# The low parts of the down-projection weights in the expert stage: from VectorE to GpSimd

## The chip, the cores and the metric

The kernel runs on one core of one Trainium2 chip. The metric is the device time of one execution in microseconds (us). Five engines of the core take part: TensorE (PE, its weight loads are PEld), VectorE (DVE), ScalarE (ACT), GpSimd (POOL) and SyncE (SP), which issues the weight loads. All weights are read from HBM once per use, 248 MB in all.

## The reference, cut to what matters

Two residual layers over 256 tokens of width 1024. Each has a token mixer (attention, gated linear attention, pooling) and then a channel mixer: a dense SwiGLU in layer 0, and in layer 1 a choice of 2 out of 8 experts for each token.

```python
def swiglu(h, w_gate, w_up, w_down):
    return (jax.nn.silu(h @ w_gate) * (h @ w_up)) @ w_down

def moe_ffn(h, w_router, w_e_gate, w_e_up, w_e_down):
    ...
    for e in range(N_EXPERTS):                      # 8
        y = y + combine[..., e:e + 1] * swiglu(h, w_e_gate[e], w_e_up[e], w_e_down[e])
    return y
```

An expert is 1024 -> 1408 -> 1024, all in float32. The change lies in this last stage, the loop over the experts.

## The kernel before, in words

**Two parts for each weight.** A float32 product is made from three faster ones in the format fp32r: a weight w is split into w_hi (w rounded to fp32r) and w_lo = w - w_hi, an activation likewise, and TensorE computes x_hi*w_hi + x_lo*w_hi + x_hi*w_lo (`three`, lines 946, 947 and 948). So every weight passes ScalarE once (`round_hi`, line 320: ring -> w_hi) and VectorE once (`rest_lo`, line 328: ring minus w_hi -> w_lo), and both parts go to TensorE.

**Units, loads and halves.** One expert is one unit of 12 loads, in the order of `UNIT_LOADS` (line 43): G0 U0 G1 U1 D0 G2 U2 D1 G3 U3 D2 D3. G is gate, U is up, D is down; groups 0 to 2 are three tiles wide (1.5 MB a load), group 3 is two tiles wide (1 MB). Each load has two halves, numbered j = 0 to 23, load j // 2. A half of a wide group is 128x1536 elements, one of group 3 is 128x1024. The down halves are j = 8, 9 (D0), 14, 15 (D1), 20, 21 (D2), all 128x1536, and 22, 23 (D3), 128x1024: 8 of the 24. In the text below, "half 8" is the half with j = 8, hi(8) is its rounding on ScalarE, lo(8) its subtraction.

**Buffers.** The ring holds four loads (load i lies in slot i % 4). There are three pairs of w_hi/w_lo buffers (`NSPLIT`), half j uses pair j % 3. The semaphores `hi_ready{b}`, `lo_ready{b}` and `split_used{b}` count them: ScalarE starts hi(j) when TensorE is done with half j - 3 (`split_used`), lo(j) starts when hi(j) is done (`hi_ready`), TensorE starts half j when both are done (`parts`, line 816), and SyncE issues the load that goes into a slot when the lo of the second half that lay there is done (`unit_read`, line 381).

**Order on each engine.** Each engine walks j = 0 to 23 in its own program order, expert after expert. What else an expert needs is hung between the halves by `EXPERT_AFTER` (line 55). On TensorE it stands right behind the half of that number: "scatter" (adding the previous expert's rows into xT, L917) behind 3 and 5, "tr" (transposes of the hidden rows, L928) behind 5, 11, 17 and 20, "gather" (the tokens of the next expert, L905) behind 19. On ScalarE and VectorE the same entries stand three halves later (`EXPERT_AFTER.get(j - NSPLIT)`), ahead of hi(j) and lo(j): "gu" is the SiLU (L1452) and the product with up (L1976), "tr" is the hidden rows' hi (L1458) and lo (L1981), "gather" the tokens' hi (L1433) and lo (L1953), "scatter" the addition into xT (L1965). All these VectorE instructions read one operand from PSUM. Only lo(j) (L328) reads both from SBUF.

**GpSimd** builds constants at the start and has elementwise work in the two token mixers, the largest being L1106 (128x2048). Its program ends with L1112, at 756 us. From there on it is idle.

Of the kernel before, what the change touches and what calls it, by code (L numbers as in the profile page):

```python
# [6 lines left out]
D, T, DEPTH, P = 1024, 256, 2, 128  # L7
# [15 lines left out]
DFF, NE, DE = 2816, 8, 1408  # L23
# [19 lines left out]
UNIT_LOADS = ["G0", "U0", "G1", "U1", "D0", "G2", "U2", "D1", "G3", "U3", "D2", "D3"]  # L43
NDENSE = DFF // UF
CAP = 96
PASSES = -(-T // CAP)

HALVES = 2 * len(UNIT_LOADS)
NSPLIT = 3
# [11 lines left out]
def scatter_use(r, e):  # L61

    return PASS_USES * r + (5 * e + 1 if not (isinstance(e, int) and e == NE) else PASS_USES - 2)


def turn_use(r, e, g, last=False):

    base = PASS_USES * r + 5 * e + 3
    return (g % 2, base + (g // 2 if g < 3 else (1 if last else 2)))
# [69 lines left out]
def hybrid_trunk(nc, A, out):  # L139
# [6 lines left out]
    with ctx:  # L146
        def sb(name, shape, dt=F32):
            return ctx.enter_context(nc.sbuf_tensor(name, shape, dt))
# [8 lines left out]
        def sem(name):  # L157
            if name not in sems:
                sems[name] = ctx.enter_context(nc.semaphore(name))
            return sems[name]  # L160
# [111 lines left out]
        npi = sb("npi", [P, 1], I32)  # L272
# [16 lines left out]
        def half_buffer(u, j):  # L289

            return j % NSPLIT, PERH * u + j // NSPLIT + 1

        def wait_hi(eng, u, j):
            b, n = half_buffer(u, j)
            eng.wait_ge(sem(f"hi_ready{b}"), n)
# [10 lines left out]
        def half_words(j):  # L306

            gn = GROUPS[int(UNIT_LOADS[j // 2][1])][1]
            n = gn * D // 2
            return n, (j % 2) * n  # L310
# [12 lines left out]
        def rest_lo(dve, u, j):  # L323

            b, _ = half_buffer(u, j)
            wait_hi(dve, u, j)
            words, w0 = half_words(j)
            dve.tensor_tensor(w_lo[:, b, 0:words], ring[:, (j // 2) % NSLOT, w0:w0 + words],  # L328
                              w_hi[:, b, 0:words].bitcast(F32), SUB).then_inc(sem(f"lo_ready{b}"), 1)
# [688 lines left out]
        def _(pool):  # L1018
# [43 lines left out]
            for L in range(DEPTH):  # L1062
# [38 lines left out]
                for a in range(TT):  # L1101
                    for d in range(2):
# [9 lines left out]
            pool.affine_select(out=tri, in_=tri, compare_op=ALU.is_ge, fill=0.0, base=-1, pattern=[[1, P]],  # L1112
                               channel_multiplier=-1).then_inc(sem("tri_ready"), 1)


        @block.scalar
        def _(act):
# [374 lines left out]
        def _(dve):  # L1492
# [454 lines left out]
            def tokens(r, e, n):  # L1947

                for c in range(2):
                    b, uses = gather_use(r, e - 1, c)  # L1950
                    dve.wait_ge(sem("hTe_hi_ready"), 2 * n + c + 1)
                    k = slice(4 * c, 4 * c + 4)
                    dve.tensor_tensor(hTe_lo[:, k, :], PS[:, 4 + b, 0:4 * CAP].rearrange("p (k c) -> p k c", k=4),  # L1953
                                      hTe_hi[:, k, :].bitcast(F32), SUB).then_inc(sem(f"aux_free{b}"), 1)

            def rows_out(n):
                wait_used(dve, NDENSE + n, HALVES - 1)
                dve.tensor_copy(ye[:, 512:1024], PS[0:CAP, 7, :]).then_inc(sem("ye_dve"), 1)

            def added(uses, part):  # L1960

                for c in (2 * part, 2 * part + 1):
                    wait_aux_full(dve, c % 2, uses + c // 2)
                    x = xT[:, 2 * c:2 * c + 2, :]
                    dve.tensor_tensor(x, x, two(PS[:, 4 + c % 2, :]), ADD).then_inc(sem(f"aux_free{c % 2}"), 1)  # L1965

            def expert(r, e, n, first=False, last=False):
                u = NDENSE + n
                for j in range(HALVES):
                    if j == 2 and not first:  # L1970
                        rows_out(n - 1)
                    for what, g in EXPERT_AFTER.get(j - NSPLIT, ()):
                        g0, gn = GROUPS[g]
                        if what == "gu":
                            dve.wait_ge(sem("sile_ready"), len(GROUPS) * n + g + 1)
                            dve.tensor_tensor(hide[:, g % 2, 0:gn * P], sile[:, g % 2, 0:gn * P],  # L1976
                                              PS[0:CAP, 2 * (g % 2) + 1, 0:gn * P], MUL).then_inc(sem("hide_ready"), 1)
                        elif what == "tr":
                            b, _ = turn_use(r, e, g, last)
                            dve.wait_ge(sem("hdT_hi_ready"), len(GROUPS) * n + g + 1)  # L1980
                            dve.tensor_tensor(hdT_lo[:, g0:g0 + gn, :],  # L1981
                                              PS[:, 4 + b, 0:gn * CAP].rearrange("p (k c) -> p k c", k=gn),
                                              hdT_hi[:, g0:g0 + gn, :].bitcast(F32), SUB).then_inc(sem(f"aux_free{b}"), 1)
                        elif what == "scatter" and not first:
                            added(scatter_use(r, e), g)
                        elif what == "gather" and not last:
                            tokens(r, e + 1, n + 1)
                    if not (j < NSPLIT and isinstance(n, int) and n == 0):
                        rest_lo(dve, u, j)

            def weigh():
# [16 lines left out]
            def one_pass(r):  # L2008
                n = r * NE
                for a in range(TT):  # L2010
                    dve.tensor_tensor(psel[:, a], slots[:, :].unsqueeze(1).broadcast_to([P, NE, CAP]),
                                      pos[:, a, :].unsqueeze(2).broadcast_to([P, NE, CAP]), ALU.is_equal)\
                       .then_inc(sem("psel_ready"), 1)
                if isinstance(r, int):
                    weigh()
                dve.wait_ge(sem("psel_ready"), 2 * (r + 1))
                for a in range(TT):
                    dve.tensor_tensor(wsel[:, a], psel[:, a], wt[:, a, :].unsqueeze(2).broadcast_to([P, NE, CAP]), MUL)\
                       .then_inc(sem("sel_ready"), 1)
                dve.tensor_scalar(pos[:, :, :], pos[:, :, :], float(CAP), None, SUB).then_inc(sem("pos_step"), 1)  # L2020
                dve.wait_ge(sem("pos_step"), r + 1)
                tokens(r, 0, n)
                expert(r, 0, n, first=True)
                with dve.Fori(1, NE - 1) as e:
                    expert(r, e, n + e)
                expert(r, NE - 1, n + NE - 1, last=True)
                rows_out(n + NE - 1)
                for part in range(2):
                    added(scatter_use(r, NE), part)
# [3 lines left out]
            npass = dve.value_load(npi[0:1, 0:1], min_val=1, max_val=PASSES)  # L2033
# [42 lines left out]
```

## Time and profile before

| what | value |
|---|---|
| time of three runs | 1362.99 us median (1362.39, 1362.99, 1373.96) |
| span of the profiled execution (first to last instruction) | 1360.9 us |
| median of the runs minus that span | 2.1 us |
| TensorE busy, share of the span | 1271.6 us, 93% |
| VectorE busy | 908.7 us, 67% |
| ScalarE busy | 720.9 us, 53% |
| GpSimd busy | 108.4 us, 8% |
| mean granted TensorE clock | 0.942 of full speed |

The span is that of one execution under the profiler; its own time is not listed apart from it, so the 2.1 us between the span and the median stand for what lies around the span. The experts fill the last third, from about 900 us to 1350 us. Busy time of TensorE is that of pipelined matmuls: the start of one to the start of the next is the better measure of what one costs (a 128x512 one starts 0.23 us after the one before, a 128x384 one 0.175 us).

### The profile page before, as it was taken

The numbers are of one execution on the slowest core, as the hardware profiler recorded it, in microseconds if no ns is written. First come the engines' busy times: TensorE is split into PE (matmuls) and PEld (weight loads), VectorE is DVE, ScalarE is ACT, GpSimd is POOL, SyncE is SP. The second block draws the span as 40 slices with busy tenths as digits, with TensorE's granted clock in tenths as the row PEclk, the third lists the DMA queues.
The fourth block names the chain that finished last, engine by engine and source line by source line (L and its number), as shares of the span: only waits on it lengthen the run. The fifth ranks groups of instructions, "written<-read, shape, count | busy, mean of one in ns | idle before, by whom it ended". The sixth has DMA issues, their size and how long they took to land.

```text
span 1360.9 us, 21645 instructions
## 1 busy us (share of the span) xinstructions
PE 1271.6 (93%) x8701; PEld 1170.2 (86%) x8701; DVE 908.7 (67%) x1130; ACT 720.9 (53%) x929; POOL 108.4 (8%) x126
## 2 busy tenths in 40 slices
PE   6999988998899999899988899889999999999997
PEld 6889878998899999879878899788888888888885
DVE  4538975577444454434896548658888788888884
ACT  4745733354444443654483235537666666666763
POOL 3005322000000000000731200000000000000000
PEclk8989977999999999997996689979999999999999
DMA  6443331245446544342342134629998988989982
GB/s 216 127 124 101 93 93 63 94 155 189 167 155 217 187 140 128 112 131 68 101 136 77 48 105 159 232 64 312 305 324 293 333 308 297 323 299 333 305 292 86
DMA packets 162662, 248.10 MB, mean 182 GB/s; under 512 B 4254, under 2 KB 140564, under 8 KB 162580
## 3 DMA queue, kind: packets, MB, share of 16 engines
q1 hardware_dynamic: 161328, 246.82, 54.2%
q8 instruction: 59, 0.97, 0.3%
q10 hardware_dynamic: 1252, 0.13, 0.1%
q14 instruction: 23, 0.19, 0.0%
HBM read 245.89 MB, written 1.05 MB: 181 GB/s over the span
## 4 chain that ended last, share of the span: by engine, by line
PE 77%; DVE 15%; ACT 4%; issue 3%; POOL 2%; DVEq 0%; POOLq 0%; ACTq 0%
PE PS L528 20%; PE PS L946 8%; PE PS L947 8%; PE PS L948 8%; PE PS L829 5%; PE PS L831 5%; PE PS L830 5%; PE PS L694 4%; DVE m_lo L1582 4%; PE PS L905 2%; PE PS L492 2%; DVE w_lo L328 2%; ACT w_hi L320 2%; DVE scr L1744 2%; PE PS L625 2%
## 5 line engine op out<-in xcount | busy, mean ns | idle before, releaser
L328 DVE TENSOR_TENSOR w_lo<-ring,w_hi 128x1536 fp32r<-128x1536 f32 (+1 forms) x240 | 388.0, 1624 | 152.9 <-ACT w_hi L320 151.4
L320 ACT ACTIVATE w_hi<-ring 128x1536 fp32r<-128x1536 f32 (+1 forms) x240 | 329.2, 1378 | 159.7 <-PE PS L831 85.9
L1178 ACT ACTIVATE m_hi<-ring 128x512 fp32r<-128x512 f32 (+2 forms) x256 | 156.6, 629 | 222.2 <-PE PS L528 221.8
L1582 DVE TENSOR_TENSOR m_lo<-ring,m_hi 128x512 fp32r<-128x512 f32 (+2 forms) x256 | 190.2, 772 | 115.4 <-ACT m_hi L1178 114.4
L528 PE MATMUL PS<-h_hi,m_hi 128*128 128x256 f32 (+2 forms) x672 | 202.9, 302 | 13.1 <-DVE h_lo L1590 7.1
L528 PE MATMUL PS<-h_lo,m_hi 128*128 128x256 f32 (+2 forms) x672 | 197.3, 294 | 0.0
L528 PE MATMUL PS<-h_hi,m_lo 128*128 128x256 f32 (+2 forms) x672 | 196.9, 293 | 0.0
L946 PE MATMUL PS<-w_hi,hTe_hi 128*96 128x384 f32 (+1 forms) x512 | 168.6, 329 | 6.7 <-DVE w_lo L328 5.5
L947 PE MATMUL PS<-w_hi,hTe_lo 128*96 128x384 f32 (+1 forms) x512 | 165.3, 323 | 0.0
L948 PE MATMUL PS<-w_lo,hTe_hi 128*96 128x384 f32 (+1 forms) x512 | 165.1, 323 | 0.0
L528 PEld LDWEIGHTS PS<-h_hi,m_hi 128*128 128x128 f32 (+2 forms) x672 | 134.7, 200 | 18.1 <-issue 12.3
L528 PEld LDWEIGHTS PS<-h_lo,m_hi 128*128 128x128 f32 (+2 forms) x672 | 134.5, 200 | 1.1 <-issue 0.5
L528 PEld LDWEIGHTS PS<-h_hi,m_lo 128*128 128x128 f32 (+2 forms) x672 | 134.2, 200 | 0.4
L829 PE MATMUL PS<-h_hi,w_hi 128*128 128x256 f32 x352 | 100.5, 285 | 2.8 <-DVE h_lo L1590 2.8
L830 PE MATMUL PS<-h_lo,w_hi 128*128 128x256 f32 x352 | 100.2, 285 | 0.0
L831 PE MATMUL PS<-h_hi,w_lo 128*128 128x256 f32 x352 | 100.1, 284 | 0.0
L946 PEld LDWEIGHTS PS<-w_hi,hTe_hi 128*96 128x96 f32 x512 | 82.6, 161 | 16.1 <-issue 10.0
L947 PEld LDWEIGHTS PS<-w_hi,hTe_lo 128*96 128x96 f32 x512 | 82.8, 162 | 5.9
L948 PEld LDWEIGHTS PS<-w_lo,hTe_hi 128*96 128x96 f32 x512 | 82.7, 162 | 5.1
L694 PE MATMUL PS<-selh,scr 128*128 128x2 f32 x256 | 55.1, 352 | 20.4 <-DVE scr L1744 20.4
L694 PEld LDWEIGHTS PS<-selh,scr 128*128 128x128 f32 x256 | 54.8, 332 | 21.1 <-issue 21.1
L946 PE MATMUL PS<-w_hi,hdT_hi 128*96 128x512 f32 x176 | 70.3, 399 | 0.9 <-issue 0.9
(310 smaller groups left out, 2451.0 us busy)
## 6 DMA issues: line engine op xcount, KB each, us to landing
ring<-in_w_in_dram SPq DMA_DIRECT2D x40, 1024.0 KB, 5.2
ring<-in_w_exp_gate_dram SPq DMA_DIRECT2D x24, 1536.0 KB, 7.8
ring<-in_w_exp_up_dram SPq DMA_DIRECT2D x24, 1536.0 KB, 8.3
ring<-in_w_exp_down_dram SPq DMA_DIRECT2D x24, 1536.0 KB, 7.3
ring<-in_w_branch_dram SPq DMA_DIRECT2D x12, 1024.0 KB, 5.0
ring<-in_w_ffn_gate_dram SPq DMA_DIRECT2D x6, 1536.0 KB, 6.6
ring<-in_w_ffn_up_dram SPq DMA_DIRECT2D x6, 1536.0 KB, 7.1
ring<-in_w_ffn_down_dram SPq DMA_DIRECT2D x6, 1536.0 KB, 6.4
```

The lines of the kernel that those rows point to most:

```text
L320: act.activation(w_hi[:, b, 0:words], ring[:, i % NSLOT, w0:w0 + words], ACT.Copy)\
L328: dve.tensor_tensor(w_lo[:, b, 0:words], ring[:, (j // 2) % NSLOT, w0:w0 + words], w_hi[:, b, 0:words].bitcast(F32), SUB).then_inc(sem(f"l ...
L528: mm = pe.matmul(dst, l, r, start=(kt == 0 and x == 0 and y == 0), stop=(kt == PIECES * per - 1 and y == 2), skip_group_check=True)
L694: mm = pe.matmul(bank[:, c * GH + 2 * d:c * GH + 2 * d + 2], E[:, d, c, :, :], selh[:, :], start=True, stop=True)
L829: pe.matmul(dst, whi, xhi, start=start, stop=False, skip_group_check=True)
L830: pe.matmul(dst, whi, xlo, start=False, stop=False, skip_group_check=True)
L831: return pe.matmul(dst, wlo, xhi, start=False, stop=stop, skip_group_check=True)
L946: pe.matmul(dst, xhi, whi, start=start, stop=False)
L947: pe.matmul(dst, xlo, whi, start=False, stop=False)
L948: return pe.matmul(dst, xhi, wlo, start=False, stop=stop)
L1178: act.activation(hi, raw, ACT.Copy).then_inc(sem("m_hi_ready"), 1)
L1582: dve.tensor_tensor(lo, raw, hi.bitcast(F32), SUB).then_inc(sem("m_lo_ready"), 1)
```

## The change

In the expert stage VectorE leaves out lo(j) for the down halves, and GpSimd runs a loop of its own that does just these, in the same order: lo(8), lo(9), lo(14), lo(15), lo(20) to lo(23) of each of the 8 experts. Instruction, operands, buffers and semaphores are the same (`rest_lo` is called with `pool` in place of `dve`). The dense stage isn't touched: there VectorE does all. The block `If(npass > 1)` serves a case (over 96 tokens for one expert) that these inputs don't reach.

```diff
@@ -1112,6 +1112,22 @@
             pool.affine_select(out=tri, in_=tri, compare_op=ALU.is_ge, fill=0.0, base=-1, pattern=[[1, P]],
                                channel_multiplier=-1).then_inc(sem("tri_ready"), 1)
 
+            def expert(n):
+
+                for j in range(HALVES):
+                    if UNIT_LOADS[j // 2][0] == "D":
+                        rest_lo(pool, NDENSE + n, j)
+
+            expert(0)
+            with pool.Fori(1, NE) as e:
+                expert(e)
+            pool.wait_ge(sem("passes_known"), 1)
+            npass = pool.value_load(npi[0:1, 0:1], min_val=1, max_val=PASSES)
+            with pool.If(npass > 1):
+                with pool.Fori(1, npass) as r:
+                    with pool.Fori(0, NE) as e:
+                        expert(r * NE + e)
+
@@ -1985,7 +2001,7 @@
                         elif what == "gather" and not last:
                             tokens(r, e + 1, n + 1)
-                    if not (j < NSPLIT and isinstance(n, int) and n == 0):
+                    if UNIT_LOADS[j // 2][0] != "D" and not (j < NSPLIT and isinstance(n, int) and n == 0):
                         rest_lo(dve, u, j)
```

## Rows read from the trace of the kernel before

**Rows 1.** Windows: us, busy by engine, then PEclk, DMA share, GB/s.

```profile
930.00:1361.00 431.00, 413.69 (x2395) 353.49 (x2393) 343.19 (x295) 275.56 (x267) 0.00 (x0) 1.00 0.86 293
1125.30:1180.80 55.50, 54.52 (x317) 46.74 (x318) 45.76 (x40) 36.77 (x36) 0.00 (x0) 1.00 0.91 312
```

**Rows 2.** Waits, 1125.3 to 1180.8 us: us in total, times, longest us.

```profile
ACT w_hi L320 <- PE PS L948: 9.2, 13, 1.9
DVE w_lo L328 <- ACT w_hi L320: 8.3, 16, 1.1
PE PS L946 <- DVE w_lo L328: 0.8, 1, 0.8
```

**Rows 3.** Timeline of TensorE, one expert: start us, us, [idle before <-releaser].

```profile
1125.30 0.41 PE L946 MATMUL PS<-w_hi,hTe_hi 128*96 128x384 f32 x1 [0.77 <-DVE w_lo L328]
...
1146.29 0.39 PE L946 MATMUL PS<-w_hi,hdT_hi 128*96 128x512 f32 x1
...
1150.45 0.34 PE L946 MATMUL PS<-w_hi,hTe_hi 128*96 128x384 f32 x1
...
1159.12 0.39 PE L946 MATMUL PS<-w_hi,hdT_hi 128*96 128x512 f32 x1
...
1163.29 0.28 PE L946 MATMUL PS<-w_hi,hTe_hi 128*96 128x256 f32 x1
...
1172.68 0.46 PE L946 MATMUL PS<-w_hi,hdT_hi 128*96 128x512 f32 x1
...
1174.95 0.45 PE L946 MATMUL PS<-w_hi,hdT_hi 128*96 128x512 f32 x1
...
1180.80 0.41 PE L946 MATMUL PS<-w_hi,hTe_hi 128*96 128x384 f32 x1 [0.77 <-DVE w_lo L328]
```

**Rows 4.** Timeline of VectorE, the same expert.

```profile
1144.10 3.58 DVE L328 TENSOR_TENSOR w_lo<-ring,w_hi 128x1536 fp32r<-128x1536 f32 x2 [0.92 <-ACT w_hi L320]
...
1148.38 3.52 DVE L328 TENSOR_TENSOR w_lo<-ring,w_hi 128x1536 fp32r<-128x1536 f32 x2 [0.25 <-ACT w_hi L320]
...
1156.92 3.58 DVE L328 TENSOR_TENSOR w_lo<-ring,w_hi 128x1536 fp32r<-128x1536 f32 x2 [0.46 <-ACT w_hi L320]
...
1160.89 1.21 DVE L328 TENSOR_TENSOR w_lo<-ring,w_hi 128x1024 fp32r<-128x1024 f32 x1
...
1168.38 3.43 DVE L328 TENSOR_TENSOR w_lo<-ring,w_hi 128x1536 fp32r<-128x1536 f32 x2 [0.73 <-ACT w_hi L320]
...
1176.51 1.23 DVE L328 TENSOR_TENSOR w_lo<-ring,w_hi 128x1024 fp32r<-128x1024 f32 x1 [0.59 <-ACT w_hi L320]
1178.80 3.43 DVE L328 TENSOR_TENSOR w_lo<-ring,w_hi 128x1536 fp32r<-128x1536 f32 x2 [1.06 <-ACT w_hi L320]
```

**Rows 5.** Timeline of ScalarE: hi(0) and hi(1) of the next expert.

```profile
1177.28 2.94 ACT L320 ACTIVATE w_hi<-ring 128x1536 fp32r<-128x1536 f32 x2 [0.80 <-PE PS L948]
```

**Rows 6.** GpSimd's lines by form: count | busy us, mean ns | idle before.

```profile
L1106 POOL TENSOR_TENSOR scr<-scr,gk 128x2048 f32<-128x2048 f32 x8 | 38.1, 4782 | 103.2 <-ACT scr L1339 103.2
...
L1084 POOL TENSOR_TENSOR kdec<-gk,PT 128x512 f32<-128x512 f32 x2 | 2.6, 1284 | 0.0
```

**Rows 7.** Timelines of VectorE and GpSimd, 169 to 186 us, in token mixer 0.

```profile
169.45 6.93 DVE L1582 TENSOR_TENSOR m_lo<-ring,m_hi 128x512 fp32r<-128x512 f32 x4
176.31 2.28 DVE L1766 TENSOR_TENSOR qk<-PS,chm 128x2048 f32<-128x2048 f32 x1
178.63 4.32 DVE L1744 TENSOR_TENSOR scr<-scr,gq 128x2048 f32<-128x2048 f32 x1
182.87 2.48 DVE L1582 TENSOR_TENSOR m_lo<-ring,m_hi 128x512 fp32r<-128x512 f32 x4
...
170.91 9.89 POOL L1106 TENSOR_TENSOR scr<-scr,gk 128x2048 f32<-128x2048 f32 x2 [23.00 <-ACT scr L1339]
```

**Rows 8.** DMA issues: count, KB each, median us from issue to landing.

```profile
ring<-in_w_exp_up_dram SPq DMA_DIRECT2D x24, 1536.0 KB, 8.3
```

**Rows 9.** Windows of 4 us in token mixer 0, columns as in rows 1.

```profile
170.00:174.00 4.00, 2.85 (x24) 2.85 (x25) 4.00 (x4) 3.97 (x6) 3.09 (x1) 1.00 0.80 239
...
182.00:186.00 4.00, 2.91 (x14) 2.94 (x15) 4.00 (x6) 0.00 (x0) 0.00 (x0) 0.64 0.00 0
```

## Prediction, made before the changed kernel was run

> **What bounds the kernel now.** I read the windows of the expert stage first: from 930 us to the end TensorE is busy 413.7 of 431 us at full granted clock (2.4 GHz), VectorE 343, ScalarE 276, GpSimd 0 [rows 1]. Then one expert: the first matmul of half 0 starts at 1125.30 and again at 1180.80, so an expert takes 55.50 us [rows 3]. In it TensorE waits for VectorE once, 0.77 us, ahead of half 0 [rows 2, 3]. ScalarE waits for TensorE (9.2 us) and VectorE for ScalarE (8.3 us): the loop runs TensorE done with half j-3, hi(j), lo(j), TensorE half j, and its pace is TensorE's [rows 2]. VectorE, busy 45.8 of 55.5 us, is not the bound. So there is little to win: all of TensorE's waits for lo in the stage are some 0.8 us for each expert. The question is whether lo of the down halves, slower on GpSimd, still comes before TensorE wants it.
>
> **Price of one lo on GpSimd.** No row shows this instruction there. The nearest are its two-input instructions of 128x512 (1.28 us) and 128x2048 (4.78 mean) [rows 6]. The mean of the second holds waits: two of them took 9.89 us while VectorE's m_lo ran beside them [rows 7]. Take 4.57, worked out here: in rows 7 VectorE's third m_lo ends at about 171.3, and the two GpSimd instructions and one m_lo (2.48/4 = 0.62) in between last until 170.91 + 9.89 = 180.80; (180.80 - 171.3 - 0.4)/2 = 4.55, rounded up a little. Through 512 and 2048 the line is 0.19 us plus 2.14 ns an element: p = 3.47 us for 128x1536, q = 2.38 us for 128x1024. Bounds: below, in proportion and without a fixed part, 4.57 x 1536/2048 = 3.43 and 2.29, with a little slack 3.35 and 2.25; above, 4.78 x 1536/2048 = 3.6, with slack for the output format fp32r, which no GpSimd row has, 3.75 and 2.6. On VectorE the same take 1.76 (3.52/2) and 1.22 [rows 4].
>
> **What is removed.** From VectorE 6 x 1.76 + 2 x 1.22 = 13.0 us for each expert. Its work isn't on the path, so this is worth nothing by itself. lo(0), the one for which TensorE waits, starts at 1178.80 when hi(0) is ready, 1.06 us after VectorE fell idle [rows 4], so an emptier VectorE doesn't bring it forward.
>
> **What is added, half by half.** I walk through the expert of rows 3 and 4, with everything ahead of the pair unchanged. From the end of a lo to TensorE's start is 0.23 us (lo(0), 1178.80 + 3.43/2 = 1180.5, against 1180.80, gives 0.28; I take 0.23). A down half takes TensorE 2.08 us ((1150.45 - 1146.29)/2).
>
> D0 (halves 8, 9). hi(8) is ready at 1144.10. lo(8) on GpSimd until 1147.57, TensorE starts half 8 at 1147.80 where it started at 1146.29: late by 1.51, ends 1149.88. lo(9) queues behind lo(8) and ends at 1151.04; half 9 starts 1151.27, ends 1153.35, where it ended at 1150.45. **+2.90 us** (in general 2p - 4.04).
>
> D1 (14, 15). Same pattern: hi(14) ready 1156.92, half 14 was wanted at 1159.12 (2.20 later, as 2.19 before), the pair was done at 1163.29. Now 1156.92 + 2p + 0.23 + 2.08 = 1166.17: **+2.88 us**.
>
> D2, D3 (20 to 23). Here the gather stands ahead of half 20 on TensorE and covers a part: hi(20) ready 1168.38, half 20 wanted only at 1172.68. But four lo's queue on GpSimd, until 1168.38 + 2p + 2q = 1180.08. Ends are 1171.85 (in time for half 20), 1175.32 (half 21 was wanted at 1174.95, late by 0.6), 1177.70, 1180.08; hi(23), ready at 1176.51 before, is there in time with 0.6 more. Half 23, 6 matmuls or 1.39 us, then runs from 1180.31 to 1181.70. Next is lo(0) of the next expert, on VectorE. hi(0) started at 1177.28, when half 21 was done [rows 5], and moves by 0.6, ready at 1179.35; with the lock (below) lo(0) starts when GpSimd is free, 1180.08, ends 1181.84, and TensorE starts half 0 at 1182.07 against 1180.80: **+1.27 us** (2p + 2q - 10.43). The 0.77 us of wait that was there hides a part.
>
> Sum for one expert 2.90 + 2.88 + 1.27 = 7.05 us (6p + 2q - 18.5), for eight 56.4; the last has no half 0 behind it and loses 1.8 in place of 1.27: 57.0 us. The stalls aren't made up again anywhere: TensorE has no other idle time in the expert to give back.
>
> **The shared read port.** Rows 7 show what VectorE does beside GpSimd. Four m_lo take 2.48 us alone, but 6.93 when GpSimd's 128x2048 runs: one of them was held for about 4.5 us, one whole GpSimd instruction. L1744 of 128x2048 took 4.32 us and ended at 182.95, 2.15 after GpSimd's pair had ended at 180.80. L1766, as large, with one operand in PSUM, took 2.28 beside GpSimd. So an instruction with two SBUF operands waits for the whole GpSimd instruction, and one with a PSUM operand doesn't. The Trainium skill, page "SBUF — State Buffer", section "Who interferes with whom", says just this: a VectorE instruction with two SBUF inputs and a GpSimd one that reads SBUF exclude each other for the whole instruction. By that rule, the trace agrees, only L328 is hit, not the other VectorE work of the stage. Priced: GpSimd holds the port 6p + 2q = 25.6 us for each expert, VectorE's remaining 16 lo's need 12 x 1.76 + 4 x 1.22 = 26.0 us, together 51.6 of the new 62.6 us, so the port isn't the bound. By place: lo(10), ready 1148.35, waits until 1151.04 and ends at 1152.80, wanted (with D0's delay) at 1153.35: hidden by 0.3. lo(16), ready 1160.89, waits until lo(15) is done at 1163.86, wanted 1166.17: hidden. lo(0): the 0.4 us counted above. If nothing excluded anything, the sum would be 0.4 x 8 = 3 us less.
>
> **Transfers.** Load 8 goes out when lo(9) is done, 3.4 us later than before, against 2.9 for TensorE. It lands 8.3 us on [rows 8], 1159.3; hi(16), its first reader, follows at about 1162.7. For D3's slot: 1180.08 + 8.3 = 1188.4, hi(6) is wanted from 1190.5. Covered by 2 to 3 us; DMA is busy 0.91 of the time and has more air at 62.6 us an expert. SyncE's wait in order adds nothing else.
>
> **Rivals.**
> A. VectorE gets in between two queued GpSimd instructions. In rows 7 the waiting m_lo did: GpSimd's second instruction came after it. Here VectorE's lo(10) would have to be ready before lo(8) ends (1148.35 against 1147.57, margin 0.8 us) or lo(16) before lo(14) ends (1160.89 against 1160.39, margin 0.5). Then the second lo of the pair is late by another 1.76 or 1.22 us: 3.0 x 8 = 24, 1444 us. It decides from p = 4.0 for D1, 4.25 for D0. Chance 0.15.
> B. The clock. The stalls (1.5, 1.4 us twice for each expert) could cost TensorE its full clock. For it: after 178 to 182 us, almost without a matmul, the granted clock was 0.64 in the window [rows 9], down to 1.2 GHz next. Against: with 2.85 busy of 4 us it stayed at 1.00 [rows 9]. A pair here has 2.1 us of work in 3.5. If one stretch of 8 us for each expert ran at half clock it would cost 8 x 8 = 64 us beyond the sum: 1484. Chance 0.07.
> C. GpSimd is quick enough: not slower. It decides from 1144.10 + 2p + 0.23 <= 1148.38, p <= 2.0 us, and for the last four 2p + 2q <= 10.4. Then nothing is late and nothing is won: 1363 us. The row of 4.78 at 2048, and 1.28 at only 512, speak against it. Chance 0.04; a gain of over 1% (14 us) isn't there to have, since TensorE's waits for lo are 8 x 0.8 = 6 us.
> D. Other, such as GpSimd well slower for fp32r (p = 4.2: 6 x 4.2 + 2 x 2.9 - 18.5 = 12.5 for each expert, at least 1463): 0.08.
>
> **How the numbers follow.** Forecast 0.66: the profile's span 1360.9 + 57.0 = 1417.9; the median of the runs is 2.1 us above the span, so 1363.0 + 57.0 = 1420.0. With p, q from 3.35, 2.25 to 3.75, 2.6 the loss for one expert is 6.1 to 9.2, so 1412 to 1437. The range takes in A (1444) and goes a little below for handoffs and D2's cover that I may have put too high: 1404 to 1450. B and most of D stay outside. This kernel's measurement can tell about 1% from no change: faster 0.01, same 0.04, slower 0.95.
>
> **What would show it.** GpSimd's L328 at about 3.5 us (128x1536) and 2.4 (128x1024), 64 in all, 205 us busy. TensorE's waits for GpSimd's w_lo: about 1.5, 1.4, 1.5, 1.4, then 0.6, 0.3, 1.0 us in each expert, and gather to gather 62.6 us in place of 55.5. Some of VectorE's L328 stretched to 3 or 4 us, above all the first after D0 and D1. Granted clock 1.00. Wrong it would be with a GpSimd lo far from 3.5 us, with VectorE's lo(10) or lo(16) between two of GpSimd's, or with the clock below 1.

## The result, and the profile after

| | before | after |
|---|---|---|
| median of the runs | 1362.69 us (4 runs, 1361.12 to 1373.96) | 1419.33 us (4 runs, 1417.24 to 1421.78) |
| ratio, 95% interval | | 1.0391 (1.0341 to 1.0441) |
| span of the profiled execution | 1360.9 us | 1415.2 us |
| mean granted TensorE clock | 0.942 | 0.947 |

The change costs 56.6 us (median against median). Two sections of the profile's page put it in the expert stage: the first line is busy time, share of the span and number of instructions, the other two are the span in 40 slices, in tenths. GpSimd (POOL) now works in the last third, and the granted clock (PEclk) keeps its level there.

```profile
PE 1279.6 (90%) x8701; PEld 1163.4 (82%) x8701; DVE 855.8 (60%) x1066; ACT 722.1 (51%) x929; POOL 312.1 (22%) x190
...
POOL 3006311000000000005312000053524335352533
PEclk9989977999999999989977899899999999999999
```

GpSimd's instructions from 900 us on, by form (count | busy us, mean ns | idle before):

```profile
L328 POOL TENSOR_TENSOR w_lo<-ring,w_hi 128x1536 fp32r<-128x1536 f32 x48 | 166.0, 3481 | 440.5 <-ACT w_hi L320 440.5
L328 POOL TENSOR_TENSOR w_lo<-ring,w_hi 128x1024 fp32r<-128x1024 f32 x16 | 38.0, 2400 | 0.0
```

So a lo on GpSimd takes 3.48 and 2.40 us, 1.76 and 1.22 on VectorE [rows 4]. One expert in windows (columns as in rows 1), from the first matmul of half 0 to the same one of the next expert: 62.39 us where it was 55.50.

```profile
1149.14:1211.53 62.39, 56.03 (x318) 46.40 (x318) 39.20 (x32) 36.92 (x36) 25.46 (x8) 1.00 0.79 278
```

TensorE's timeline in that expert, which answers to rows 3. Shown are the first matmuls of halves 8, 9, 10, then 14, 15, 16, then 20, 21, 23 and 0 (start us, us, [idle before <-releaser]):

```profile
1171.82 0.44 PE L946 MATMUL PS<-w_hi,hdT_hi 128*96 128x512 f32 x1 [1.54 <-POOL w_lo L328]
...
1175.06 0.45 PE L946 MATMUL PS<-w_hi,hdT_hi 128*96 128x512 f32 x1 [0.94 <-POOL w_lo L328]
...
1177.20 0.34 PE L946 MATMUL PS<-w_hi,hTe_hi 128*96 128x384 f32 x1
...
1187.30 0.44 PE L946 MATMUL PS<-w_hi,hdT_hi 128*96 128x512 f32 x1 [1.29 <-issue]
...
1190.78 0.44 PE L946 MATMUL PS<-w_hi,hdT_hi 128*96 128x512 f32 x1 [1.18 <-POOL w_lo L328]
...
1192.91 0.28 PE L946 MATMUL PS<-w_hi,hTe_hi 128*96 128x256 f32 x1
...
1202.32 0.45 PE L946 MATMUL PS<-w_hi,hdT_hi 128*96 128x512 f32 x1
...
1205.11 0.44 PE L946 MATMUL PS<-w_hi,hdT_hi 128*96 128x512 f32 x1 [0.33 <-POOL w_lo L328]
...
1209.81 0.44 PE L946 MATMUL PS<-w_hi,hdT_hi 128*96 128x512 f32 x1 [0.62 <-POOL w_lo L328]
...
1211.53 0.41 PE L946 MATMUL PS<-w_hi,hTe_hi 128*96 128x384 f32 x1
```

Half 0 began at 1125.30 before and at 1149.14 after, so 23.84 us bring the two onto one scale. Half 10 was to start at 1150.45 + 23.84 = 1174.29 and started at 1177.20: 2.91 us lost on D0. Half 16: 1163.29 + 23.84 + 2.91 = 1190.04, started 1192.91: 2.87 on D1. The next half 0: 1180.80 + 23.84 + 5.78 = 1210.42, started 1211.53: 1.11 on D2 and D3. Together 6.89 us. The idle times in brackets are a little shorter than the delay, since a matmul's record reaches past the start of its successor.

GpSimd and VectorE side by side around D0 and around D2, D3:

```profile
1167.99 6.92 POOL L328 TENSOR_TENSOR w_lo<-ring,w_hi 128x1536 fp32r<-128x1536 f32 x2 [20.71 <-ACT w_hi L320]
...
1198.05 11.62 POOL L328 TENSOR_TENSOR w_lo<-ring,w_hi 128x1536 fp32r<-128x1536 f32 x4 [7.42 <-ACT w_hi L320]
...
1172.20 5.99 DVE L328 TENSOR_TENSOR w_lo<-ring,w_hi 128x1536 fp32r<-128x1536 f32 x2 [0.82 <-ACT w_hi L320]
...
1208.98 3.98 DVE L328 TENSOR_TENSOR w_lo<-ring,w_hi 128x1536 fp32r<-128x1536 f32 x2 [3.44 <-ACT w_hi L320]
```

The queue of two runs from 1167.99 to 1174.91, and half 9 starts 0.15 us after it. lo(10) on VectorE has its operands at 1172.20 but lasts 4.32 us, until 1176.52: it is held until GpSimd is done at 1174.91 and then takes 1.6. TensorE wants it at 1177.20, so this holding is hidden. At the end of the expert lo(0), begun at 1208.98, waits for GpSimd's last (1209.67) in the same way; this one isn't hidden.

### The profile page after: what moved, and what is told of

Read it like the earlier page. It is cut to its first block, busy times and chain, and to the rows that moved or that the text cites. A ratio compares the mean times of both kernels' runs of the same rounds, so it can differ in the third digit from the quotient of the medians.

```text
span 1415.2 us, 21700 instructions
## 1 busy us (share of the span) xinstructions
PE 1279.6 (90%) x8701; PEld 1163.4 (82%) x8701; DVE 855.8 (60%) x1066; ACT 722.1 (51%) x929; POOL 312.1 (22%) x190
## 3 DMA queue, kind: packets, MB, share of 16 engines
q1 hardware_dynamic: 161328, 246.82, 51.4%
## 4 chain that ended last, share of the span: by engine, by line
PE 50%; issue 22%; POOL 14%; DVE 12%; ACT 2%; POOLq 0%; DVEq 0%; ACTq 0%
PE PS L528 20%; POOL w_lo L328 12%; PE PS L829 5%; PE PS L830 5%; PE PS L831 5%; PE PS L694 4%; DVE m_lo L1598 3%; PE PS L492 2%; DVE scr L1760 2%; PE PS L625 1%; PE PS L739 1%; DVE small L1720 1%; PE PS L501 1%; DVE Pr L1732 1%; DVE w_lo L328 1%
## 5 line engine op out<-in xcount | busy, mean ns | idle before, releaser
L328 DVE TENSOR_TENSOR w_lo<-ring,w_hi 128x1536 fp32r<-128x1536 f32 (+1 forms) x176 | 331.1, 1894 | 156.1 <-ACT w_hi L320 156.0
L328 POOL TENSOR_TENSOR w_lo<-ring,w_hi 128x1536 fp32r<-128x1536 f32 (+1 forms) x64 | 203.7, 3211 | 440.5 <-ACT w_hi L320 440.5
L1072 POOL TENSOR_TENSOR qk<-qk,rows 32x512 f32<-32x512 f32 x8 | 12.7, 1613 | 527.5 <-PE PS L656 527.5
L946 PEld LDWEIGHTS PS<-w_hi,hdT_hi 128*96 128x96 f32 x176 | 28.3, 161 | 80.1 <-issue 72.2
```

Of the source, the lines that this page charges most:

```text
L946: pe.matmul(dst, xhi, whi, start=start, stop=False)
```

## The experiments

Each time stands beside that of the kernel before on the same chip; except for the last, each is a single run. "Period" is gather to gather in the profile (first L905 of one expert to the next), 55.50 us before and 62.38 after. "Stage" is from the first gather to the end of the span. Both are read to 0.1 us where the time of a single run isn't: the first gather comes anywhere from 893 to 908 us, in code that no experiment touches, and that enters the times.

| run | time, us more than before | stage, us | more than before |
|---|---|---|---|
| kernel before | | 464.2 | |
| changed kernel | 56.6 | 522.2 | 58.0 |
| half of the instructions | 19.8 | 487.9 | 23.7 |
| only D2 and D3 | 9.4 | 475.9 | 11.7 |
| short instruction | 2.8 | 464.2 | 0.0 |
| same duration without reading | 51.4 | 517.6 | 53.4 |
| unneeded reads | 94.9 | 557.8 | 93.6 |
| unneeded writes | 1.5 | 464.1 | -0.1 |
| longer lo | 196.6 | 648.1 | 183.9 |
| half 0 in two instructions | -4.9 | 460.1 | -4.1 |

The diffs are shortened to the lines that matter. In all runs with GpSimd work but the one with only D2 and D3, its loop over the experts is also written out (`for e in range(NE)`) in place of `Fori`; with the unneeded writes this leaves the period at 55.50.

The theory: TensorE waits because the lo's of a down pair stand in one GpSimd queue, p = 3.5 us each, behind a hi that comes no earlier than before; what is lost is read from each place by what covers it. Rivals: the cost goes with GpSimd's time of work (its hold on the shared read port); the hand-over to another engine or the later release of ring slots costs; VectorE gets in between; the clock falls.

### Half of the instructions moved

```diff
-    if UNIT_LOADS[j // 2][0] == "D":
+    if UNIT_LOADS[j // 2][0] == "D" and j % 2 == 1:
```

VectorE takes the rest. GpSimd's lo(9) also waits for VectorE's lo(8) here, so that the load's slot is freed by both.

> Only the second halves of the down loads (9, 15, 21, 23) go to GpSimd, the first ones (8, 14, 20, 22) stay on VectorE. Theory (a queue of two GpSimd instructions makes the pair late): lo(8) is in time on VectorE, lo(9) starts on GpSimd with it done, 1145.9 + 3.48 + 0.23 = 1149.6 against 1148.4 wanted: 1.2 us late; D1 the same; D2's lo(21) is covered by the gather; D3 0.1. Together 2.5 us for each expert, +20 us, period 58.0 us. Rival (cost in proportion to the time that GpSimd works, because it holds the shared port or because of handing over): half of the 56.6 us measured, +28 us, spread over all four.

Measured: 1384.9 us against 1365.0, +19.8 us; period 58.26 us, 2.76 more than before. Half the instructions cost 40% of the loss of a period (and 41% of that of the stage); the rival wanted half. That is a narrow margin, and the next run separates the two better. TensorE waits for GpSimd's w_lo in 20 instances of about 0.9 us in the 390 us from 950 on (18.3 us in all).

```profile
PE PS L946 <- POOL w_lo L328: 18.3, 20, 1.2
```

These are three in an expert, by place: 1.1 us at D0, 1.1 at D1 and 0.5 at D3, where 0.1 was expected. With the first lo of a pair on VectorE, the second alone is still late: one GpSimd lo is too slow where TensorE follows at once.

### Only D2 and D3 moved

```diff
-    if UNIT_LOADS[j // 2][0] == "D":
+    if UNIT_LOADS[j // 2] in ("D2", "D3"):
```

> Only the halves 20 to 23 (D2 and D3) go to GpSimd, D0 and D1 stay on VectorE. Theory: place decides. The gather on TensorE covers most of the queue of four, so the loss is the 1.1 us measured there for each expert, +9 us, period 56.6 us. Rival (cost in proportion to GpSimd's busy time, 11.8 of 25.5 us for each expert): 46% of 56.6 us, +26 us.

Measured: 1374.4 against 1365.0, +9.4 us; period 56.56, 1.06 more than before. 46% of GpSimd's time of work causes 15% of the loss for one expert, the same 1.1 us that D2 and D3 lose in the changed kernel. Cost in proportion to GpSimd's work falls (it wanted 26 us, the stage shows 11.7); place decides. The stage's 11.7 are 7 x 1.06 and 4.3 in the last expert, which the expected +9 had left out. The queue of four is there as before:

```profile
1172.74 11.60 POOL L328 TENSOR_TENSOR w_lo<-ring,w_hi 128x1536 fp32r<-128x1536 f32 x4 [44.94 <-ACT w_hi L320]
```

### The same waits and signals with a short instruction

```diff
-    rest_lo(pool, NDENSE + n, j)
+    wait_hi(pool, NDENSE + n, j)
+    pool.memset(w_lo[:, b, 0:words].bitcast(F32), 0.0).then_inc(sem(f"lo_ready{b}"), 1)
```

> GpSimd fills w_lo of the down halves with zeros in place of the subtraction (the low parts of the down weights are left out of the result), so the same waits, signals and queue but about 1.4 us for 128x1536, write only. Theory (only the duration matters, decided at p = 2.0 us): nothing late, 1361 to 1364 us, period 55.5 us. Rival (handing over to GpSimd, or slots freed later): part of the 7 us for each expert remains.

Measured: 1367.9 against 1365.0 in one run each; period 55.53 us, that of the kernel before to 0.03. GpSimd's lines there, and TensorE's waits, which are those of the kernel before:

```profile
L1123 POOL MEMSET w_lo<- 128x1536 f32 x42 | 58.0, 1382 | 286.4 <-ACT w_hi L320 286.4
L1123 POOL MEMSET w_lo<- 128x1024 f32 x14 | 13.3, 953 | 31.0 <-ACT w_hi L320 31.0
```

```profile
PE PS L946 <- DVE w_lo L328: 5.5, 7, 0.8
```

The 2.8 us lie ahead of the experts: the stage takes 464.2 us in both profiles. So the hand-over to GpSimd costs nothing at 1.4 us, below the point of decision of 2.0 us, which itself was not tested. A later release of the ring's slots is not tested here, since a lo of 1.4 us frees them no later; it is in the next run. This one also shows that nothing is to be won: VectorE loses the down lo's, and the period stays.

### The same duration without reading

Two more memsets into the unused m_lo tile ahead of the one above, so that a lo takes 3.34 us (start to start) and 2.49 us, but GpSimd reads nothing.

```diff
+    step(pool.memset(spare, 0.0))                      # 128 x words
+    step(pool.memset(spare[:, 0:words // 1024], 0.0))  # 128 x 512
     pool.memset(w_lo[:, b, 0:words].bitcast(F32), 0.0).then_inc(sem(f"lo_ready{b}"), 1)
```

> As the one with zeros, but with two more memsets into a scratch tile ahead, so that each lo takes about 3.4 us (128x1536) and 2.4 us (128x1024) and GpSimd never reads SBUF (the low parts of the down weights are left out). Theory: the stalls of TensorE return almost whole, period 62.0 us, +54 us; only lo(0) of the next expert is no longer held, 0.4 us less for each expert, and no L328 of VectorE lasts longer than 1.8 us. Rival (the shared port is the main cause): far less, under +20 us.

Measured: 1416.4 against 1365.0, +51.4 us; period 61.73 us. The stalls are back though the port is free: VectorE's longest L328 (its durations are min/median/max in ns) is 1.76 us, against 4.33 in the changed kernel, whose row stands second.

```profile
L328 DVE TENSOR_TENSOR w_lo<-ring,w_hi x101: 1224/1758/1761, 949.4 to 1339.3; 128x1536 fp32r<-128x1536 f32 x76, 128x1024 fp32r<-128x1024 f32 x25
```

```profile
L328 DVE TENSOR_TENSOR w_lo<-ring,w_hi x99: 1211/1758/4325, 959.4 to 1338.2; 128x1536 fp32r<-128x1536 f32 x75, 128x1024 fp32r<-128x1024 f32 x24
```

The formula with these durations gives 6 x 3.34 + 2 x 2.49 - 18.5 = 6.5 us, and 6.1 with nothing held; measured 6.2. The slots are freed nearly as late here as in the changed kernel, and the formula, which has no term for that, leaves at most 0.1 us for it. Of the 6.88 us for each expert at most 0.65 are due to the port (62.38 - 61.73, of which about 0.4 is the shorter duration).

### The port alone: unneeded reads, unneeded writes

The kernel before, in which VectorE does every lo, with GpSimd working on tiles nobody uses, at the same moments.

```diff
+    wait_hi(pool, NDENSE + n, j)
+    step(pool.tensor_tensor(m_lo[:, 0:words // 512, 0:512], x, x, SUB))   # x = m_hi, in SBUF
```

> The kernel before, where VectorE does every lo, plus a GpSimd that does an unneeded subtraction of the same size, both operands in SBUF, each time hi of a down half is ready. Nobody waits for it. Theory of the shared read port: VectorE's lo(9), lo(10) and so on are held for whole GpSimd instructions of 3.5 us, TensorE becomes late by about 5 to 6 us at D0 and D1 each and at D2/D3 together, 16 us for each expert, +100 to +150 us, and L328 rows of 4 to 5 us on VectorE. Rival (no exclusion): the time of the kernel before, 1363 us.

Measured: 1456.5 against 1361.6, +94.9 us; period 66.63 us, 11.1 more. Direction and mechanism as expected, the size a third smaller: I had every GpSimd instruction hold a lo that TensorE waits for, but VectorE's lo came first each time and the two engines took turns, and at D0 two held lo's made TensorE late, 1.69 us for lo(9) and 1.87 for lo(10):

```profile
1195.05 0.44 PE L946 MATMUL PS<-w_hi,hdT_hi 128*96 128x512 f32 x1 [1.69 <-DVE w_lo L328]
...
1199.22 0.39 PE L946 MATMUL PS<-w_hi,hTe_hi 128*96 128x384 f32 x1 [1.87 <-issue]
```

The 11.1 us are waits of this kind, and nothing of them is the clock: the same two waits, to 0.04 us, stand in all eight experts, and in five of the six periods (66.62 to 66.64 us) the granted clock is 1.00. Only in the expert shown, and in the last one, did it fall right after them, here in windows of 4 us (columns as in rows 1). This period took 68.22 us, 1.6 more than the others:

```profile
1196.00:1200.00 4.00, 2.13 (x11) 1.39 (x10) 4.00 (x2) 1.48 (x1) 1.51 (x1) 1.00 0.89 261
1200.00:1204.00 4.00, 4.00 (x16) 3.51 (x15) 2.69 (x3) 1.48 (x1) 0.00 (x0) 0.59 0.52 126
```

With memsets of 1.4 + 1.4 + 0.5 us in place of the subtraction:

```diff
-    step(pool.tensor_tensor(m_lo[:, 0:words // 512, 0:512], x, x, SUB))
+    step(pool.memset(x, 0.0)), step(pool.memset(x, 0.0)), step(pool.memset(x[:, 0:words // 1024], 0.0))
```

> As the one with unneeded reads, but GpSimd's instructions are memsets of the same total duration (about 3.4 and 2.4 us), write only. Theory: only reading excludes VectorE's two-operand instructions, so 1363 us and no L328 over 1.8 us on VectorE. Rival (any GpSimd instruction blocks): again +100 us.

Measured: 1363.1 against 1361.6 in one run each; period 55.50 us, exactly that of before, and VectorE's longest L328 is 1.76 us. The exclusion is one of reads: GpSimd's reading holds VectorE's subtraction, its writing doesn't. With the waits that it sets off it is worth about 94 us where VectorE's lo's stand close to TensorE's need, and 5 us at most (8 x 0.65) in the changed kernel, where they have moved out of the way.

### A longer lo

```diff
+    step(pool.tensor_tensor(m_lo[:, 0, 0:512], x, x, SUB))    # 128x512, unneeded
     rest_lo(pool, NDENSE + n, j)
```

> The changed kernel with an unneeded GpSimd subtraction of 128x512 (1.3 us) ahead of each of its eight lo's, so p is about 4.9 and q 3.8 us. Theory by the formula alone (6p + 2q - 18.5): 18.5 us for each expert, +148 us. With VectorE getting in between (rival A of the prediction, which decides from p = 4.0 and 4.25): lo(10) and lo(16) go ahead of a queued GpSimd instruction, 3 us more, +170 us, and the timelines show an L328 of VectorE between two instructions of a GpSimd pair.

Measured: 1558.2 against 1361.6, +196.6 us, of which 183.9 are in the stage (the first gather came at 908.20 us, in place of 896.75); period 78.5 us, 23.0 more, above both numbers. The added instruction takes 1.04 us alone. From one lo to the next in the queue p is 4.5 and q 3.5, and the formula gives 6 x 4.5 + 2 x 3.5 - 18.5 = 15.5. GpSimd and VectorE at D0:

```profile
1169.62 3.45 POOL L328 TENSOR_TENSOR w_lo<-ring,w_hi 128x1536 fp32r<-128x1536 f32 x1
1173.03 2.55 POOL L1124 TENSOR_TENSOR m_lo<-m_hi 128x512 fp32r<-128x512 f32 x1
1175.66 3.44 POOL L328 TENSOR_TENSOR w_lo<-ring,w_hi 128x1536 fp32r<-128x1536 f32 x1
...
1172.71 1.97 DVE L328 TENSOR_TENSOR w_lo<-ring,w_hi 128x1536 fp32r<-128x1536 f32 x1 [0.82 <-ACT w_hi L320]
```

lo(10) is ready at 1172.71, 0.36 us before GpSimd's lo(8) ends (1173.07), and goes next: GpSimd's 128x512 takes 2.55 us in place of 1.04. That is rival A of the prediction, 1.5 us here and 1.0 at D1 (2.02 against 1.04). It occurs a third time, which neither the prediction nor this run's expectation had: at the end of the expert lo(0) of the next one goes ahead of GpSimd's last lo, which takes 3.74 us in place of 2.38.

```profile
1141.76 1.03 POOL L1124 TENSOR_TENSOR m_lo<-m_hi 128x512 fp32r<-128x512 f32 x1
1142.87 3.74 POOL L328 TENSOR_TENSOR w_lo<-ring,w_hi 128x1024 fp32r<-128x1024 f32 x1
...
1142.32 2.09 DVE L328 TENSOR_TENSOR w_lo<-ring,w_hi 128x1536 fp32r<-128x1536 f32 x1 [5.21 <-ACT w_hi L320]
```

That makes 3.9 us for rival A, less about 0.5, since half 0 no longer waits for a held lo(0). The rest, 23.0 - 15.5 - 3.4 = 4.1 us for each expert, lies with rival B. Windows of 4 us in the same expert as D0 above (columns as in rows 1):

```profile
1166.00:1170.00 4.00, 3.87 (x24) 3.61 (x25) 1.13 (x3) 3.06 (x3) 1.43 (x2) 1.00 0.87 272
1170.00:1174.00 4.00, 1.37 (x8) 0.90 (x7) 1.84 (x2) 2.08 (x3) 4.00 (x2) 1.00 0.41 164
1174.00:1178.00 4.00, 2.82 (x8) 1.36 (x6) 0.68 (x1) 1.09 (x1) 3.92 (x2) 0.53 0.00 0
1178.00:1182.00 4.00, 2.76 (x7) 1.89 (x8) 2.28 (x1) 0.40 (x1) 1.09 (x1) 0.50 0.35 86
```

After a stretch with TensorE busy 1.37 of 4 us the granted clock is at its lower level (1.2 GHz). Half 9 took 3.9 us (1179.24 to 1183.16) in place of 2.1. Read the same way from the starts of matmuls, the lower level cost 0.6 us more at the start of half 10, 1.1 in half 23 and 0.5 at the start of half 0, together 4.0 us on TensorE's path: the rest is the clock.

### A version that beats both

The short memset showed that the down lo's are not what VectorE needs relief from. TensorE's one wait for a lo in an expert is the 0.77 us ahead of half 0 [rows 3], where hi(0) and lo(0) stand in series. Without GpSimd, for experts 1 to 7:

```diff
+    # ScalarE, j == 0: two instructions of 128x768, the first signals hi_first
+    act.activation(w_hi[:, b, 0:x], ring[:, s, 0:x], ACT.Copy).then_inc(sem("hi_first"), 1)
+    act.activation(w_hi[:, b, x:words], ...).then_inc(sem(f"hi_ready{b}"), 1)
+    # VectorE, j == 0
+    dve.wait_ge(sem("hi_first"), n)
+    dve.tensor_tensor(w_lo[:, 0, 0:x], ring[:, 0, 0:x], w_hi[:, 0, 0:x].bitcast(F32), SUB)
+    wait_hi(dve, u, 0)
+    dve.tensor_tensor(w_lo[:, 0, x:2 * x], ...).then_inc(sem("lo_ready0"), 1)
```

> No GpSimd work: the kernel before, where hi(0) and lo(0) of experts 1 to 7 are each done in two instructions of 128x768, so that VectorE starts on the first part 0.7 us earlier. Theory (TensorE's only avoidable wait in the expert stage is the 0.77 us ahead of half 0, which hangs on hi(0) then lo(0) in series): lo(0) ends about 0.7 us earlier, the wait nearly goes, lo(2) still comes in time to 0.2 us, period 54.9 to 55.1 us, 3 to 5 us faster than before. Rival (TensorE is held by something else there, or lo(2) is late instead): period 55.5 us, no change.

Measured: median 1357.6 us (11 runs) against 1362.5 (16 runs), ratio 0.9962 (95% interval 0.9943 to 0.9981). The period is 54.9 us, and the wait is down from 0.8 to 0.2 or 0.3 us:

```profile
PE PS L952 <- DVE w_lo L2000: 1.5, 7, 0.3
```

So 4.9 us, 0.36%, faster than the kernel before by the medians (the interval reaches from 0.2 to 0.6%, the stage shows 4.1 us), and by the medians some 62 us faster than the changed one (1419.3).

## Why the prediction was right, step by step

**Price of one lo.** 3.47 and 2.38 us were read off a line through two other GpSimd instructions [rows 6]; 3.48 and 2.40 came out. The output format fp32r, for which the upper bound had slack, added nothing to it. Taking the held instruction's wait out of the 4.78 us [rows 7] mattered: in proportion to the mean it would have been 3.6, and 0.7 us more for each expert.

**The walk.** D0 2.90 predicted, 2.91 measured; D1 2.88 and 2.87; D2 with D3 1.27 and 1.11. The last is mis-sized by 0.16: I let lo(0) take its whole 1.76 us after GpSimd's release, but a held instruction finished 1.6 us after it, and the queue of four took 11.62 us where I had 11.70. TensorE's waits, forecast at 1.5, 1.4, 1.5, 1.4, then 0.6, 0.3 and 1.0, came at the same halves but one: 1.54, 0.94, 1.29, 1.18, then 0.33, none and 0.62 in brackets. The period was to be 62.6, it is 62.4.

**The step that failed: the last expert.** The sum gave it 1.8 us for D2 and D3 in place of 1.27, and left the cover of the gather in it. But the last expert has no gather (`not last` in the code), so nothing covers the queue of four there. TensorE's timeline of the last expert after, first matmul of halves 20 and 21 (their records say what was waited for; "issue" stands where the profile shows no releaser):

```profile
1388.75 0.44 PE L946 MATMUL PS<-w_hi,hdT_hi 128*96 128x512 f32 x1 [2.62 <-issue]
...
1392.24 0.44 PE L946 MATMUL PS<-w_hi,hdT_hi 128*96 128x512 f32 x1 [1.02 <-POOL w_lo L328]
...
1399.35 3.94 PE L917 MATMUL PS<-qk,big 96*128 96x256 f32 x16 [0.82 <-ACT big L1455]
```

From the last gate/up matmul triple's start (1385.62) to the last scatter (1399.35) are 13.7 us, before 9.6 (1335.45 to 1345.03): 4.15 us lost there, 2.3 more than in the sum.

**The sum.** Over the stage, from the first gather to the end of the span: 5.8 up to the second gather, 6 periods of 6.87 = 41.2, and 10.95 from the last gather to the end (1.1 + 2.9 + 2.9 + 4.15), 58.0 us. The span grew by 54.3 only, because the profiled execution after reached its first gather 3.7 us earlier (893.04 against 896.75 us), in code that the change doesn't touch. So 57.0 predicted stands against 58.0 in the stage and 56.6 in the medians. That 1420.0 met 1419.3 to 0.7 us is in part luck: the last expert was 2.3 us too low in the sum, the other seven together about 1 us too high, and the medians have 1.4 us less than the stage.

**Nothing gained from VectorE.** Right, and shown by the short memset, which frees VectorE of the same work and leaves the period at 55.53.

**The shared read port.** With GpSimd reading beside VectorE's lo's a period took 66.63 us, with it writing 55.50. That is how the Trainium skill, page "SBUF — State Buffer", section "Who interferes with whom", tells the two apart: a VectorE instruction with two SBUF inputs contends with a GpSimd instruction that reads SBUF, and not with one that only writes it. The prediction's "not the bound, hidden except for lo(0)" was right: 0.65 us at most.

**Transfers.** Right: median time from issue to landing even fell (7.5 us for the up weights, 8.3 before [rows 8]), and no ScalarE wait for a load stands in the expert.

**Rivals.** A did not occur in the changed kernel (GpSimd's pairs run without a gap, 6.92 us for two). But it does occur with p = 4.5, and the rule by which it decides, ready before GpSimd's current instruction ends, is seen there. It was priced at 3.0 us for each expert and cost 3.4, since lo(0) gets in as well. B did not occur either: the expert's granted clock is 1.00. It occurs with the longer lo, where it cost 4.0 us for each expert; the prediction's 8 us for one stretch at half clock came from no row. C, decided at p = 2.0, is what the short memset shows at 1.4 us.

## What to carry to other kernels

An engine that is busy but waits for others in the loop is not worth relieving: look first at how long the critical engine waits for it (0.8 us in 55.5), which is all there is to win. Moving work to an engine half as fast costs, for each place, the queue's end minus what covers it; walk one period through by its start times, place by place, and then separately the first and the last round, where the cover may be missing. A VectorE instruction with both operands in SBUF should not stand close to its deadline beside a GpSimd one that reads.

## What the runs showed of the hardware

- GpSimd's two-input instructions fit 0.19 us plus 2.14 ns an element of each partition at 1024 (2.40 us) and 1536 (3.48), subtractions with output in fp32r, and at 2048 (4.56), the shortest of the float32 multiplications at L1106 before, whose durations in ns (min/median/max) stand below. At 128x512 it was 1.04 us when both operands were the same tile, against 1.28 in rows 6; which of the two a plain one takes stays open. A memset of 128x1536 took 1.38 us, 128x1024 0.95, 128x512 0.53.

```profile
L1106 POOL TENSOR_TENSOR scr<-scr,gk x8: 4557/4782/5002, 170.9 to 749.2; 128x2048 f32<-128x2048 f32 x8
```

- A held VectorE instruction of 128x1536 ended 1.6 us after GpSimd's record where it takes 1.76 alone. Whether 0.15 us of it ran ahead of the hold is open, as the ends of GpSimd's records are rough.
- At the end of a GpSimd instruction, a VectorE instruction that already waited went ahead of GpSimd's next one, though that one's operands were ready too (lo(10) in the run with the longer lo). With no VectorE instruction waiting at that moment a pair of GpSimd's ran without a gap (6.92 us for two).
- The length of a stall alone did not decide whether TensorE's granted clock fell. In the changed kernel stalls of 1.5 and 0.9 us with 2 us of work between left it at 1.00, and so did one of 2.62 us in the last expert. In the run with the same duration without reading, the same place had a stall of 2.55 us, and the next window was at 0.57; the two windows stand below (columns as in rows 1). Stalls of 1.7 and 1.9 us (the unneeded reads) left it at 1.00 in six experts of eight. With the longer lo, with stalls of 2.4 to 3.1 us, it fell in every expert. What else decides stays open, and with it how near the changed kernel came to rival B.

```profile
1388.00:1392.00 4.00, 2.47 (x11) 1.66 (x11) 0.36 (x1) 0.74 (x2) 4.00 (x2) 1.00 0.00 0
...
1388.00:1392.00 4.00, 4.00 (x14) 2.63 (x13) 0.26 (x1) 0.62 (x2) 3.83 (x5) 0.57 0.00 0
```
